# Two small products per step: from one VectorE instruction of two columns to ScalarE copies of one column each

## The chip, the cores and the metric

One NeuronCore of a Trainium2 chip runs the whole program. Its engines are named as in the profile: PE (TensorE matmul), PEld (TensorE weight load), DVE (VectorE), ACT (ScalarE), POOL (GpSimd), SP (SyncE, which here only issues transfers). An engine name with a q is its instruction queue issuing DMAs. The metric is the device time of one execution in microseconds; the median of several executions is compared. For this kernel a change is told from no change when it is over about 0.2%, some 8 us.

## The reference

A transformer block of depth 2 (FFN, mixer, FFN) on 512 tokens of width 1024 is followed by a second block, whose last part is a product-key expert layer ("PEER"). The change touches only that part. Cut to it:

```python
scores = einsum("thpd,hpkd->thpk", query, sub_keys)      # 8 heads, 2 halves, 128 keys
...                                                      # top 16 of each, then top 16 pairs
gate = softmax(best)                                     # 512 tokens x 8 heads x 16 experts
def block_fn(tb, ib, gb):
    act = gelu(einsum("td,thkd->thk", tb, u_tab[ib]))    # u_tab, v_tab: 16384 rows of 1024
    return einsum("thk,thkd->td", gb * act, v_tab[ib])
```

Everything is float32. Each token picks 128 of 16384 experts; an expert is one row of `u_tab` and one of `v_tab`.

## The kernel before

**Two ways through the experts.** For 416 of the 512 tokens (`DENSE`) the kernel computes all experts: PE multiplies the tokens by the whole table `u` ("ahead" tiles), ACT takes the gelu into `stage` and stores it to `s_store` in HBM; later groups of 512 experts read it back (`s_in`) with their gates (`g_in`), DVE multiplies the two (`weighed`), the product is split into a high part (`w_mix_hi`, ACT) and a low part (`w_mix_lo`, DVE), and PE multiplies them by the table `v`. For the other 96 tokens (`FETCHED`) only the chosen rows are fetched, with indirect DMAs from POOL's queue: one fetch brings 128 rows of `u` and `v` (1 MB) into `fetched`, one expert slot per partition. 64 of these tokens have 64 slots per partition, 2 for each of the 32 groups (`PER_GROUP`); the other 32 tokens are the "late" ones with 32 slots, 2 for each of 16 late steps.

**A late step** `s` (`score_late`, `gelu_late`, `add_late`): DVE takes the dot products of two fetched rows with the token (`late_score`, line L3116), ACT takes their gelu (`late_gelu`, L1290), DVE multiplies the two columns by their gates (`late_factor`, L3122) and adds two scaled `v` rows to a total in PSUM (L3126). There are three sets of two `fetched` buffers, so POOL may issue the fetches of step `s + 3` when the two adds of step `s` are done. The late steps run in a window in which PE computes the last 14 ahead tiles, 28 rows of work (a row fills one PSUM bank).

**A group** `g` (`early_step` on ACT, `early_group` on DVE) does the same to two fetched slots with `slot_score` (L3090), `slot_gelu` (L1263), `slot_factor` (L3098) and `fetched_sum` (L3104), between the products `weighed` (L3064) and `w_mix_lo` (L3071). Groups 1 to 30 stand in loops on every engine.

**Weights** come as 331 tiles of 128x2048 in two buffers `raw`. SP loads a tile when POOL is done with the one that was there; ACT copies it rounded into `w_hi` (`split_hi`, L730); POOL subtracts, in four pieces of 512 columns, into `w_lo` (L563); PE waits for the pieces. Each product is then three matmuls (L1362 to L1364).

**What sets the order.** Each engine runs a list written by hand. On ACT, in the window, the gelu of late step `s` is placed after row `ceil(3 + 1.4 s)`:

```python
for row in range(2 * (AHEAD_TILES - WINDOW_AT)):
    n = WINDOW_AT + row // 2
    stage_row(n, row % 2)             # gelu of a PSUM bank, L1168
    if row % 2:
        store_tile(n)                 # DMA s_store, then split_hi of the tile after next
    while s < LATE_STEPS and 3 + 1.4 * s <= row:
        gelu_late(s)
        s += 1
    if row == 2 * (AHEAD_TILES - WINDOW_AT) - 3:
        ...
        load_group(0)                 # DMAs g_in (L1248) and s_in (L1250)
```

On POOL the tile subtractions of the window are placed between the fetches: `fetch_late(s)` first, its two waits included, then `low_tile`. `c.step(ins)` means that the engine waits for its own instruction through a semaphore before it goes on.

Of the kernel before, what the change touches and what calls it, by code (L numbers as in the profile page):

```python
# [23 lines left out]
ALU = mybir.AluOpType  # L24
ACT = mybir.ActivationFunctionType
# [54 lines left out]
PER_GROUP = SLOTS // GROUPS  # L80
# [56 lines left out]
def build(nc, x_in, weights, gains, small, pool_w, consts, rope, second, level_masks,  # L137
# [3 lines left out]
    with stack:  # L141
# [564 lines left out]
        def _(act):  # L706
# [384 lines left out]
            def experts():  # L1091
# [167 lines left out]
                def gelu_fetched(g, i=None):  # L1259

                    at = since("slots_scored") + LATE_SLOTS + PER_GROUP * (g + 1)
                    act.wait_ge(sem("slots_scored"), at if i is None else i * (2 * PER_GROUP) + at)
                    c_sg.up(act.activation(slot_gelu[:, g % 2, :], slot_score[:, g % 2, :], ACT.Gelu))  # L1263
# [12 lines left out]
                def looped(trips, g, body):  # L1276

                    with act.Fori(0, trips) as i:
                        c_wh.loop(i, 2 * EG)
                        c_sg.loop(i, 2)  # L1280
                        body(g, i)
                        body(g + 1, i)
                    for c in (c_wh, c_sg):
                        c.end(trips)

                def gelu_late(s):

                    act.wait_ge(sem("slots_scored"), since("slots_scored") + 2 * (s + 1))
                    c_sg.up(act.activation(late_gelu[:, s % 2, :], late_score[:, s % 2, :], ACT.Gelu))  # L1290

                s = 0
# [978 lines left out]
        def _(dve):  # L2271
# [625 lines left out]
            def experts():  # L2897
# [195 lines left out]
                def factor_fetched(g, i=None):  # L3093

                    done = since("slots_gelu") + LATE_STEPS + g + 1
                    dve.wait_ge(sem("slots_gelu"), done if i is None else i * 2 + done)
                    at = g if i is None else i * 2 + g
                    local.step(dve.tensor_tensor(slot_factor[:, g % 2, :], slot_gelu[:, g % 2, :], slot_gate[:, at, :],  # L3098
                                                 ALU.mult))
# [19 lines left out]
                def add_late(s):  # L3119

                    dve.wait_ge(sem("slots_gelu"), since("slots_gelu") + s + 1)
                    local.step(dve.tensor_tensor(late_factor[:, s % 2, :], late_gelu[:, s % 2, :], late_gate[:, s, :],  # L3122
                                                 ALU.mult))
# [5 lines left out]
                def early_group(g, i=None):  # L3129
# [8 lines left out]
                    factor_fetched(g, i)  # L3138
# [3 lines left out]
                def looped(trips, g, body):  # L3142

                    with dve.Fori(0, trips) as i:
# [4 lines left out]
                        local.loop(i, 2)  # L3149
                        body(g, i)  # L3150
                        body(g + 1, i)
                    for c in (c_wg, c_wl, c_ss, c_fa, local):
                        c.end(trips)
# [175 lines left out]
```

## Time and profile before

| | |
|---|---|
| median of 3 runs | 3894.67 us (3893.44 to 3897.62) |
| the profiled execution | 3893.74 us, span 3891.9 us |
| PE busy | 3771.2 us (97%) |
| DVE busy | 2111.6 us (54%) |
| ACT busy | 1399.0 us (36%) |
| POOL busy | 1978.0 us (51%) |
| granted TensorE clock, mean | 0.985 |
| late window | about 3118 to 3270 us of the span |
| groups | about 3278 to 3874 us |

The span runs from the first to the last instruction of the profiled execution. Busy shares are means over stages with different limits; the change lies in the last fifth of the span, so views of those stretches are read below. In a row of a view, "idle before <- X" is how long the engine had done nothing before the instruction and what ended that.

### The profile page before, as it was taken

The numbers are of one execution on the slowest core, as the hardware profiler recorded it, in microseconds if no ns is written. First come the engines' busy times: TensorE is split into PE (matmuls) and PEld (weight loads), VectorE is DVE, ScalarE is ACT, GpSimd is POOL, SyncE is SP. The second block draws the span as 40 slices with busy tenths as digits, with TensorE's granted clock in tenths as the row PEclk, the third lists the DMA queues.
The fourth block names the chain that finished last, engine by engine and source line by source line (L and its number), as shares of the span: only waits on it lengthen the run. The fifth ranks groups of instructions, "written<-read, shape, count | busy, mean of one in ns | idle before, by whom it ended". The sixth has DMA issues, their size and how long they took to land.

```text
span 3891.9 us, 57381 instructions
## 1 busy us (share of the span) xinstructions
PE 3771.2 (97%) x21920; PEld 3290.5 (85%) x21920; DVE 2111.6 (54%) x3552; ACT 1399.0 (36%) x2131; POOL 1978.0 (51%) x1520
## 2 busy tenths in 40 slices
PE   8999999999999999999999978999999987999998
PEld 7888778888888887788877767889999987999998
DVE  3212555220322056432124855439899968999997
ACT  4222253222322133432232433334477722333332
POOL 4444424444444442444443322546644465888885
PEclk9999999999999999999999988999999998999999
DMA  3222212222222221222223210234456699888885
GB/s 140 97 97 100 77 64 98 97 97 97 95 94 94 104 88 58 92 92 97 98 103 76 44 36 24 99 108 157 154 206 209 226 381 357 326 319 324 323 319 189
DMA packets 160292, 570.02 MB, mean 146 GB/s; under 512 B 19456, under 2 KB 85248, under 8 KB 105344
## 3 DMA queue, kind: packets, MB, share of 16 engines
q1 hardware_dynamic: 49392, 351.29, 25.7%
q10 hardware_dynamic: 96912, 115.76, 8.7%
q0 software_dynamic: 13824, 100.67, 6.3%
q8 instruction: 116, 1.90, 0.2%
q14 instruction: 48, 0.39, 0.0%
HBM read 510.93 MB, written 56.66 MB: 146 GB/s over the span
## 4 chain that ended last, share of the span: by engine, by line
issue 34%; POOL 26%; PE 24%; DVE 13%; ACT 1%; ACTq 1%; DMA 0%; POOLq 0%; DVEq 0%
POOL w_lo L563 25%; PE bank L1362 7%; PE bank L1364 7%; PE bank L1363 7%; DVE g_buf L3043 3%; DVE hot_parts L3025 2%; DVE hot_first L3026 1%; DVE hot_parts L3031 1%; DVE bank L3126 1%; DVE late_factor L3122 1%; DVE fetched L3116 1%; POOL fetched L657 1%; ACT w_hi L730 1%; DVE gk L2601 0%; PE bank L1904 0%
## 5 line engine op out<-in xcount | busy, mean ns | idle before, releaser
L563 POOL TENSOR_TENSOR w_lo<-raw,w_hi 128x512 fp32r<-128x512 f32 x1324 | 1807.6, 1396 | 1722.4 <-ACT w_hi L730 1695.0
L1362 PE MATMUL bank<-h_hi,w_hi 128*128 128x512 f32 (+1 forms) x3232 | 1235.9, 382 | 35.8 <-POOL w_lo L563 22.9
L1363 PE MATMUL bank<-h_lo,w_hi 128*128 128x512 f32 (+1 forms) x3232 | 1222.1, 378 | 0.0
L1364 PE MATMUL bank<-h_hi,w_lo 128*128 128x512 f32 (+1 forms) x3232 | 1222.1, 378 | 0.0
L730 ACT ACTIVATE w_hi<-raw 128x2048 fp32r<-128x2048 f32 x331 | 632.7, 1911 | 832.0 <-PE bank L1364 765.4
L1362 PEld LDWEIGHTS bank<-h_hi,w_hi 128*128 128x128 f32 x3232 | 609.9, 189 | 132.5 <-POOL w_lo L563 34.1
L1363 PEld LDWEIGHTS bank<-h_lo,w_hi 128*128 128x128 f32 x3232 | 610.1, 189 | 89.7 <-issue 3.4
L1364 PEld LDWEIGHTS bank<-h_hi,w_lo 128*128 128x128 f32 x3232 | 609.4, 189 | 88.8
L1362 PE MATMUL bank<-w_mix_hi,w_hi 128*128 128x416 f32 x1024 | 363.3, 355 | 16.0 <-DVE w_mix_lo L3071 15.0
L1364 PE MATMUL bank<-w_mix_hi,w_lo 128*128 128x416 f32 x1024 | 361.8, 353 | 0.0
L1363 PE MATMUL bank<-w_mix_lo,w_hi 128*128 128x416 f32 x1024 | 358.9, 350 | 0.0
L2318 DVE SCALAR_TENSOR_TENSOR x<-bank,x 128x512 f32<-128x512 f32 x56 | 38.1, 680 | 451.1 <-PE bank L1364 451.1
L1364 PE MATMUL bank<-act_hi,w_lo 128*128 (+1 forms) x704 | 274.1, 389 | 0.0
L1362 PE MATMUL bank<-act_hi,w_hi 128*128 (+1 forms) x704 | 274.1, 389 | 0.0
L1363 PE MATMUL bank<-act_lo,w_hi 128*128 (+1 forms) x704 | 274.1, 389 | 0.0
L2354 DVE TENSOR_TENSOR up_s<-bank,rstd 128x512 f32<-128x512 f32 x88 | 60.8, 691 | 381.6 <-PE bank L1364 381.3
L765 ACT ACTIVATE act_hi<-up_s 128x512 f32 (+1 forms) x88 | 55.6, 632 | 458.7 <-DVE up_s L2356 458.7
L1362 PEld LDWEIGHTS bank<-w_mix_hi,w_hi 128*128 128x128 f32 x1024 | 192.9, 188 | 24.0 <-issue 17.6
L3071 DVE TENSOR_TENSOR w_mix_lo<-weighed,w_mix_hi 128x416 fp32r<-128x416 f32 x128 | 199.7, 1560 | 6.9 <-ACT w_mix_hi L1257 3.0
L1363 PEld LDWEIGHTS bank<-w_mix_lo,w_hi 128*128 128x128 f32 x1024 | 193.4, 189 | 2.7
L1364 PEld LDWEIGHTS bank<-w_mix_hi,w_lo 128*128 128x128 f32 x1024 | 193.0, 189 | 1.3
L3064 DVE TENSOR_TENSOR weighed<-s_in,g_in 128x416 f32<-128x416 f32 x128 | 156.6, 1243 | 13.2 <-DMA s_in<-s_store 11.0
(430 smaller groups left out, 4416.4 us busy)
## 6 DMA issues: line engine op xcount, KB each, us to landing
raw<-weights SPq DMA_DIRECT2D x331, 1024.0 KB, 4.8
s_store<-stage ACTq DMA_DIRECT2D x64, 416.0 KB, 4.7
g_store<-g_buf ACTq DMA_DIRECT2D x8, 3328.0 KB, 15.4
g_in<-g_store ACTq DMA_DIRECT2D x32, 832.0 KB, 6.7
s_in<-s_store ACTq DMA_DIRECT2D x32, 832.0 KB, 8.2
x<-x_in SPq DMA_DIRECT2D x4, 512.0 KB, 8.5
out<-x SPq DMA_DIRECT2D x8, 256.0 KB, 2.2
q_mask<-rows ACTq DMA_DIRECT2D x6, 256.0 KB, 4.3
```

The costliest lines, as they stand in the source:

```text
L563: pool.tensor_tensor(w_lo[:, slot, cols], raw[:, slot, cols], w_hi[:, slot, cols].bitcast(F32), ALU.subtract).then_inc(lo_written, 1)
L657: pool.indirect_dma_start(out=fetched[b][:, :, :].rearrange("p a d -> p (a d)"), out_offset=None, in_=expert_rows, in_offset=bass.Indirect ...
L730: act.activation(w_hi[:, slot, :], raw[:, slot, :], ACT.Copy).then_inc(hi_written, 1)
L765: c_act_hi.up(act.activation(act_hi[:, at, :], prod[:, :], ACT.Copy))
L1362: pe.matmul(out_ap, w_hi[:, slot, cols], m_hi, start=start, stop=False)
L1363: pe.matmul(out_ap, w_hi[:, slot, cols], m_lo, start=False, stop=False)
L1364: return pe.matmul(out_ap, w_lo[:, slot, cols], m_hi, start=False, stop=stop)
L2354: c_us.step(dve.tensor_tensor(up_s[:, :], banks[up_bank][:, :], rstd[:, :], ALU.mult))
L3025: local.up(dve.tensor_tensor(parts[:, :, 0:P], every, over_keys(chosen[:, 0]), ALU.is_equal))
L3043: ins = dve.tensor_reduce(g_buf[:, c % 2, :, at:at + 2], both, AX_X, ALU.add)
L3064: c_wg.up(dve.tensor_tensor(chunked(weighed[:, e % 2, :]), chunked(s_in[:, slot, e, :]), g_in[:, slot, :, e, :], ALU.mult))
L3071: c_wl.step(dve.tensor_tensor(w_mix_lo[:, g % 2, e, :], weighed[:, e % 2, :], w_mix_hi[:, g % 2, e, :].bitcast(F32), ALU.subtract))
```

## The change

The gate product leaves DVE. After each gelu of two columns, ACT waits for its own result and then writes the factor as two copies of one column, each scaled by the gate of its slot through a per-partition operand; the semaphore on which DVE waited for the gelu is raised by the second copy. DVE has no product and no wait for its own product any more; `await_factor` is the bare wait.

```diff
                     act.wait_ge(sem("slots_scored"), at if i is None else i * (2 * PER_GROUP) + at)
-                    c_sg.up(act.activation(slot_gelu[:, g % 2, :], slot_score[:, g % 2, :], ACT.Gelu))
+                    act_local.step(act.activation(slot_gelu[:, g % 2, :], slot_score[:, g % 2, :], ACT.Gelu))
+                    at = g if i is None else i * 2 + g
+                    for j in range(PER_GROUP):
+                        ins = act.activation(slot_factor[:, g % 2, j:j + 1], slot_gelu[:, g % 2, j:j + 1], ACT.Copy,
+                                             scale=slot_gate[:, at, j:j + 1])
+                    c_sg.up(ins)
...
                     act.wait_ge(sem("slots_scored"), since("slots_scored") + 2 * (s + 1))
-                    c_sg.up(act.activation(late_gelu[:, s % 2, :], late_score[:, s % 2, :], ACT.Gelu))
+                    act_local.step(act.activation(late_gelu[:, s % 2, :], late_score[:, s % 2, :], ACT.Gelu))
+                    for j in range(2):
+                        ins = act.activation(late_factor[:, s % 2, j:j + 1], late_gelu[:, s % 2, j:j + 1], ACT.Copy,
+                                             scale=late_gate[:, s, j:j + 1])
+                    c_sg.up(ins)
...
-                def factor_fetched(g, i=None):
+                def await_factor(g, i=None):
 
                     done = since("slots_gelu") + LATE_STEPS + g + 1
                     dve.wait_ge(sem("slots_gelu"), done if i is None else i * 2 + done)
-                    at = g if i is None else i * 2 + g
-                    local.step(dve.tensor_tensor(slot_factor[:, g % 2, :], slot_gelu[:, g % 2, :], slot_gate[:, at, :],
-                                                 ALU.mult))
...
                     dve.wait_ge(sem("slots_gelu"), since("slots_gelu") + s + 1)
-                    local.step(dve.tensor_tensor(late_factor[:, s % 2, :], late_gelu[:, s % 2, :], late_gate[:, s, :],
-                                                 ALU.mult))
```

On ACT, at the end of the late window, the list of before reads as follows (`z_read` is the semaphore that counts the scores, and `s_ahead_done` and `tile_used` count PE's rows):

```order
1271 L1290 ACTIVATE late_gelu<-late_score 128x2 [waits z_read]
1272 L1168 ACTIVATE stage<-bank 128x416 [waits s_stored0,s_ahead_done]
1273 L1290 ACTIVATE late_gelu<-late_score 128x2 [waits z_read]
1274 L1168 ACTIVATE stage<-bank 128x416 [waits tile_used]
1275 L1173 DMA s_store<-stage 128x832 [waits s_staged]
1276 L730 ACTIVATE w_hi<-raw 128x2048 [waits tile_used,tile_landed1]
1277 L1248 DMA g_in<-g_store 128x8x208 [waits gates_stored1,gates_stored0]
1278 L1250 DMA s_in<-s_store 128x2x832
```

and that of the change:

```order
1299 L1296 ACTIVATE late_gelu<-late_score 128x2 [waits z_read]
1300 L1298 ACTIVATE late_factor<-late_gelu,late_gate 128x1 [waits act_local]
1301 L1298 ACTIVATE late_factor<-late_gelu,late_gate 128x1
1302 L1168 ACTIVATE stage<-bank 128x416 [waits s_stored0,s_ahead_done]
1303 L1296 ACTIVATE late_gelu<-late_score 128x2 [waits z_read]
1304 L1298 ACTIVATE late_factor<-late_gelu,late_gate 128x1 [waits act_local]
1305 L1298 ACTIVATE late_factor<-late_gelu,late_gate 128x1
1306 L1168 ACTIVATE stage<-bank 128x416 [waits tile_used]
1307 L1173 DMA s_store<-stage 128x832 [waits s_staged]
1308 L730 ACTIVATE w_hi<-raw 128x2048 [waits tile_used,tile_landed1]
1309 L1248 DMA g_in<-g_store 128x8x208 [waits gates_stored1,gates_stored0]
1310 L1250 DMA s_in<-s_store 128x2x832
```

Nothing but the two copies per gelu, the first with a wait on ACT's own semaphore, has come in; the places of the gelus, of `stage`, of `w_hi` and of the first group's two loads are the same, and no load of a function table is added.

On DVE, at the last two late steps (`v_new_written` counts what ACT hands over, `dve_local` is DVE's wait for itself, `x_written2` counts the adds; the number behind `fetched` tells the buffer), before:

```order
1815 L3122 TENSOR_TENSOR late_factor<-late_gelu,late_gate 128x2 [waits v_new_written]
1816 L3126 SCALAR_TENSOR_TENSOR bank<-fetched_193,late_factor,bank 128x1024 [waits x_written2,dve_local]
1817 L3126 SCALAR_TENSOR_TENSOR bank<-fetched_194,late_factor,bank 128x1024 [waits x_written2]
1818 L3116 SCALAR_TENSOR_TENSOR fetched_195,late_score<-fetched_195,bank 128x1024 [waits fetched_landed2]
1819 L3116 SCALAR_TENSOR_TENSOR fetched_196,late_score<-fetched_196,bank 128x1024 [waits fetched_landed3]
1820 L3122 TENSOR_TENSOR late_factor<-late_gelu,late_gate 128x2 [waits v_new_written]
1821 L3126 SCALAR_TENSOR_TENSOR bank<-fetched_195,late_factor,bank 128x1024 [waits x_written2,dve_local]
```

and of the change:

```order
1801 L3131 SCALAR_TENSOR_TENSOR bank<-fetched_193,late_factor,bank 128x1024 [waits x_written2,v_new_written]
1802 L3131 SCALAR_TENSOR_TENSOR bank<-fetched_194,late_factor,bank 128x1024 [waits x_written2]
1803 L3123 SCALAR_TENSOR_TENSOR fetched_195,late_score<-fetched_195,bank 128x1024 [waits fetched_landed2]
1804 L3123 SCALAR_TENSOR_TENSOR fetched_196,late_score<-fetched_196,bank 128x1024 [waits fetched_landed3]
1805 L3131 SCALAR_TENSOR_TENSOR bank<-fetched_195,late_factor,bank 128x1024 [waits x_written2,v_new_written]
```

The product is gone and the wait for ACT has moved to the first add.

## Rows read from the trace of the kernel before

**Rows 1.** Three stretches: length, busy PE, PEld, DVE, ACT, POOL, clock, DMA share, GB/s.

```profile
3150.00:3256.00 106.00, 93.46 (x472) 91.01 (x471) 94.84 (x87) 30.65 (x43) 73.18 (x66) 0.95 1.01 408
3256.00:3264.00 8.00, 8.00 (x44) 7.88 (x43) 7.66 (x11) 0.61 (x2) 6.81 (x6) 1.00 0.53 201
...
3290.00:3860.00 570.00, 569.02 (x2991) 557.57 (x2991) 543.34 (x466) 189.57 (x218) 465.65 (x305) 1.00 0.83 312
```

**Rows 2.** Waits by engine, 3110 to 3300 us: total us, times, longest us.

```profile
ACT late_gelu L1290 <- DVE fetched L3116: 50.8, 14, 5.9
...
PE bank L1362 <- POOL w_lo L563: 20.2, 4, 7.7
...
PE bank L1362 <- DVE w_mix_lo L3071: 15.0, 1, 15.0
```

**Rows 3.** DVE's instruction groups, 3157 to 3257 us: busy us, mean ns, idle before.

```profile
L3122 DVE TENSOR_TENSOR late_factor<-late_gelu,late_gate 128x2 f32<-128x2 f32 x13 | 34.2, 2632 | 10.6 <-ACT late_gelu L1290 10.6
L3126 DVE SCALAR_TENSOR_TENSOR bank<-fetched,late_factor,bank 128x1024 f32<-128x1024 f32 x26 | 33.5, 1290 | 0.9
L3116 DVE SCALAR_TENSOR_TENSOR fetched<-fetched,bank 128x1024 f32<-128x1024 f32 x25 | 29.5, 1215 | 0.0
```

**Rows 4.** Timeline around two late steps: start, us, instruction, idle before.

```profile
3235.53 0.16 DVE L3122 TENSOR_TENSOR late_factor<-late_gelu,late_gate 128x2 f32<-128x2 f32 x1 [0.27 <-ACT late_gelu L1290]
3235.73 2.62 DVE L3126 SCALAR_TENSOR_TENSOR bank<-fetched,late_factor,bank 128x1024 f32<-128x1024 f32 x2
...
3239.57 4.98 POOL L563 TENSOR_TENSOR w_lo<-raw,w_hi 128x512 fp32r<-128x512 f32 x4
...
3240.65 0.20 ACT L1290 ACTIVATE late_gelu<-late_score 128x2 f32<-128x2 f32 x1 [4.74 <-DVE fetched L3116]
...
3240.89 3.69 DVE L3122 TENSOR_TENSOR late_factor<-late_gelu,late_gate 128x2 f32<-128x2 f32 x1 [0.27 <-ACT late_gelu L1290]
```

**Rows 5.** ACT's groups by shape, whole span: with and without a per-partition scale.

```profile
L1193 ACT ACTIVATE hot_parts<-hot_parts,gate_hi 128x128 fp32r<-128x128 f32 x416 | 129.8, 388 | 56.6 <-DVE hot_parts L3031 56.6
...
L1045 ACT ACTIVATE prod_y<-bank 128x128 f32<-128x128 f32 x32 | 8.6, 277 | 48.6 <-PE bank L1944 48.2
...
L1290 ACT ACTIVATE late_gelu<-late_score 128x2 f32<-128x2 f32 x16 | 3.2, 202 | 50.8 <-DVE fetched L3116 50.8
```

**Rows 6.** A stretch of 10 us in the late window, columns as in the first group.

```profile
3160.00:3170.00 10.00, 10.00 (x55) 10.00 (x54) 9.66 (x10) 3.15 (x4) 7.90 (x8) 1.00 1.02 426
```

**Rows 7.** DMA issues, 3190 to 3250 us: median us from issue to landing.

```profile
fetched<-expert_rows,late_at POOLq DMA_INDIRECT x16, 8.5
```

**Rows 8.** Timeline, last late fetch to first group: POOL, DVE, ACT, ACT's queue.

```profile
3247.49 0.94 POOL L657 DMA_INDIRECT fetched<-expert_rows,late_at  x1 [0.37 <-DVE bank L3126]
...
3262.24 1.21 DVE L3116 SCALAR_TENSOR_TENSOR fetched<-fetched,bank 128x1024 f32<-128x1024 f32 x1
...
3264.64 0.20 ACT L1290 ACTIVATE late_gelu<-late_score 128x2 f32<-128x2 f32 x1 [5.55 <-DVE fetched L3116]
...
3266.51 2.96 ACTq L1250 DMA_DIRECT2D s_in<-s_store  x1
...
3278.04 1.94 DVE L3064 TENSOR_TENSOR weighed<-s_in,g_in 128x416 f32<-128x416 f32 x2 [8.09 <-DMA s_in<-s_store]
```

**Rows 9.** Timeline of one group: DVE, then two rows of ACT.

```profile
3615.56 0.82 DVE L3098 TENSOR_TENSOR slot_factor<-slot_gelu,slot_gate 128x2 f32<-128x2 f32 x1 [0.34 <-DVE w_mix_lo L3071]
...
3612.06 0.20 ACT L1263 ACTIVATE slot_gelu<-slot_score 128x2 f32<-128x2 f32 x1 [0.59 <-DVE fetched L3090]
...
3617.61 1.92 ACT L730 ACTIVATE w_hi<-raw 128x2048 fp32r<-128x2048 f32 x1 [5.34 <-PE bank L1364]
```

**Rows 10.** Waits by engine in the groups, 3300 to 3860 us.

```profile
ACT w_hi L730 <- PE bank L1364: 200.3, 41, 6.7
...
PEld bank L1362 <- POOL w_lo L563: 4.5, 11, 0.5
```

**Rows 11.** Timeline, PE, the longest of its waits for `w_lo`.

```profile
3142.25 0.71 PE L1362 MATMUL bank<-h_hi,w_hi 128*128 128x416 f32 x1 [7.71 <-POOL w_lo L563]
```

More of the change, by code:

```diff
@@ L1280, in looped @@
                         c_sg.loop(i, 2)
+                        act_local.loop(i, 2)
                         body(g, i)
                         body(g + 1, i)
-                    for c in (c_wh, c_sg):
+                    for c in (c_wh, c_sg, act_local):
                         c.end(trips)
@@ L3137, in early_group @@
                             score_fetched(g, e, i)
-                    factor_fetched(g, i)
+                    await_factor(g, i)
                     for j in range(PER_GROUP):
@@ L3148, in looped @@
                             c.loop(i, 2 * PER_GROUP)
-                        local.loop(i, 2)
                         body(g, i)
                         body(g + 1, i)
-                    for c in (c_wg, c_wl, c_ss, c_fa, local):
+                    for c in (c_wg, c_wl, c_ss, c_fa):
                         c.end(trips)
```

## Prediction

> **What bounds the kernel now.** I read three views in this order: the stretches, the waits, the timeline.
>
> The stretches [rows 1] cut the last fifth of the span into parts with different limits. In the groups, 3290 to 3860 us, PE is busy 569.02 of 570 us at full clock: PE bounds them, and what DVE or ACT saves there is worth nothing unless PE waited for it. In the late window before them PE is not the bound: it is busy 93.46 of 106 us, DVE 94.84, and the DMA share is 1.01. Two limits lie close together there, DVE's chain and the DMA engines. From 3256 to 3264 us the DMA share falls to 0.53.
>
> The waits [rows 2] say where PE's idle time comes from: 20.2 us for weights that POOL had not split, and 15.0 us in one piece for the first group's `w_mix_lo`, between the last ahead row and the first group. ACT stands 50.8 us before late gelus, waiting for DVE's dot products. So DVE's chain paces ACT, and through the order on ACT and POOL also PE.
>
> DVE's groups in the window [rows 3] show what is odd: 13 factors of two columns take 34.2 us, 2632 ns each, more than the 26 adds of 1024 columns (33.5 us). The timeline [rows 4] shows why. The factor at 3235.53 takes 0.16 us. The one at 3240.89 takes 3.69 us and ends at 3244.58, just when POOL's block of four `w_lo` pieces ends (3239.57 + 4.98 = 3244.55). 
>
> The Trainium skill says this too ("SBUF — State Buffer", "Who interferes with whom"): a DVE instruction with two SBUF inputs contends with a GpSimd instruction that reads SBUF, and the loser waits for the whole instruction. By that rule the wait would be one piece, at most 4.98 / 4 = 1.25 us, and DVE would gain 1.2 us per blocked step; the trace shows 3.5 us more than the free factor, across three pieces. The measurement decides, and the sum goes by it.
>
> **The change, part by part.**
>
> *Removed in the window.* 13 factors go: 34.2 us of DVE, of which 13 x 0.16 = 2.1 us is work and 32.1 us is standing behind POOL [rows 3].
>
> *Added in the window.* Per late step ACT waits for its own gelu and makes two copies of one column with a per-partition scale. No row has such a copy. The small gelu takes 202 ns; a per-partition scale is the difference between 388 and 277 ns at 128 columns, 0.11 us [rows 5]. So one copy is some 0.31 us: two are 0.31 us if they overlap wholly and 0.62 if not at all. I take 0.5, since both are independent, plus a hop that DVE's own step (0.04 us between factor and add [rows 4]) also had. A step that was blocked gets 3.69 + 0.04 - 0.5 = 3.2 us shorter, a free one 0.3 to 0.4 us longer. For the 13 steps: 34.2 + 0.5 - 6.5 = about 28 us less in DVE's chain.
>
> The Trainium skill speaks against the move: "ScalarE: Activation LUTs", "Rules for kernel authors", puts multiplication on VectorE, and its section "What ACT_TABLE_LOAD costs" prices an ACTIVATE at 186 ns plus 0.83 ns a column plus 93 ns per pointer operand, back-to-back ones overlapping by 93 ns. An estimate from that page is 0.47 us for two copies, so by it alone each step would be 0.3 us longer than with a free factor; it leaves out what POOL does to the factor.
>
> *What of the 28 us reaches the end.* Very little, I think, because the DMA engines stand next in line. From 3150 to 3256 us they moved 408 GB/s at a share of 1.01 [rows 1], and the best 10 us of the window 426 at 1.02 [rows 6]. All that moves in it (32 fetches, the weight tiles, the stores) must still move before the first group. 106 us x 408 / 426 = 101.5 us: at most 4.5 us to be had there, nothing at the other end, and I take 0, since the share says that no engine was idle and the difference is in what was being moved.
>
> What is free is the hole after it. Fetches land 8.5 us after issue [rows 7]. The last late one is issued at 3247.49, so its rows are there at about 3256; DVE gets to them only at 3262.24, 6.2 us later [rows 8]. With 28 us out of its chain DVE will have caught up and wait for the landing instead. The last gelu (3264.64) and the load of the first group's `s_in` (3266.51) come earlier by as much as the hole allows. In the 8 us from 3256 the DMA share is 0.53: 8 x 0.47 = 3.8 us of free DMA time [rows 1]. I take 3.8 us of the 6.2: the same bytes then land with 3.8 us less idle time, and `s_in`, on which DVE waited 8.09 us until 3278.04, lands that much earlier. PE's 15.0 us wait keeps its length, because the ahead rows before it move as well: PE's 20.2 us of waits for POOL, which stood behind DVE's adds, give way. If they don't, row 25 (the one ahead of the loads on ACT) holds the load back; that is the lower end, 0.
>
> *The groups.* DVE loses a factor and its wait, 0.82 + 0.34 us in the one shown [rows 9]; ACT gains two copies. DVE then waits for the copies instead: gelu at 3612.06 + 0.20, copies to 3612.8, with 0.3 us more for register work in the loop to 3613.1, while `w_mix_lo` runs to 3615.56 - 0.34 = 3615.22. Hidden by 2 us. Behind the copies on ACT stands `w_hi`, which idles 5.34 us for PE: hidden by 4.8 us. Had those covers gone, 0.8 us for each of 30 groups would be 24 us. What is late in PE's eyes is only POOL's `w_lo`: 4.5 us in 11 waits [rows 10]. I take 0 here.
>
> *Sum.* The profiled execution took 3893.74 us, 0.9 below the median. 3893.74 - 3.8 = 3889.9; against the median 3894.67 - 3.8 = **3890.9 us**, 0.1% faster, which a measurement of this kernel (0.2%, some 8 us) can hardly tell from no change.
>
> **The rivals.**
>
> *Mostly not DMA-bound.* The share of 1.01 may hide slack. Then DVE's chain shortens by its 28 us until PE is the bound: PE's waits for weights are 20.2 us, of which the longest, 7.7 us, ends at 3142 us, ahead of the late steps that this part is about, and stays [rows 11]: 12.5 us. With the hole, 16 us: 3878.5 us. For it: DVE idles 0.0 us before its dot products [rows 3]. Against it: the share, over 106 us.
>
> *Groups with less contention.* One DVE product fewer reads beside POOL, and the 4.5 us in 11 waits for `w_lo` go: 3890.9 - 4.5 = 3886.4 us. For it: `w_lo` and DVE's products slow each other. Against it: only one small product in nine goes.
>
> *Groups with more contention, slower.* DVE now runs some 1 us ahead of POOL in each group, and its long products fall on POOL's pieces where they didn't. PE waits in 11 of about 31 groups, 0.41 us each; if all had such a wait it would be 31 x 0.41 - 4.5 = 8.2 us more. Against the gain of 3.8: 3899.1 us; without that gain 3902.9. It decides from 10 more groups with a wait on. For it: POOL is busy 465.65 of 570 us, and its tile path is what PE waits for. Against it: PE waited at most 0.5 us.
>
> *Nothing.* PE's rows hold the first group's load back, or the longer ACT step does: 3894.7 us.
>
> **How the numbers follow.** The tail gain 0.48, nothing 0.19, less contention in groups 0.12, not DMA-bound 0.11, more contention 0.10. Range: 3883 to 3899. Its upper end takes in nothing and most of more contention; its lower end takes in less contention and the 4.5 us in the window (3890.9 - 4.5 - 4.5 is 3881.9, just under it), and leaves out the case not bound by DMA. Outside it lie 0.11 and half of more contention, with the edges some 0.2. Faster by over 0.2% (below 3886.9) needs the DMA rival or less contention: 0.11 + 0.08, with some of the tail case 0.25. Slower by over 0.2% (over 3902.5): 0.06. The same: 0.69.
>
> **What would show it.** In the profile of the change: no 3.7 us instruction on DVE in the window; DVE's dot products L3123 waiting for DMAs of `fetched`; late steps no closer than 7 us on average; the DMA share 1.0 from 3150 until the first group's loads and no hole near 3256; `weighed` of the first group starting near 3274; PE's waits for `w_lo` in the groups near 4.5 us. It is wrong if late steps come at 6 us or less, if the groups' part (first `weighed` to the end) changes by more than 2 us, or if the copies take over 0.62 us together.

## The result: 0.3% slower

| | before | changed |
|---|---|---|
| median of 7 runs each, us | 3895.78 (3893.44 to 3897.62) | 3908.57 (3906.37 to 3911.01) |
| profiled execution, us | 3893.74 | 3910.09 |
| its span, us | 3891.9 | 3908.3 |
| ratio of the runs | | 1.0032, 95% interval 1.0023 to 1.0042 |

The forecast was 3890.9 us with a range of 3883 to 3899. The time lies 9.6 us above that range, on the side to which I had given 0.06.

Three marks that both traces have cut the 16.4 us between the two spans. The memset ahead of the late steps starts at 3112.14 us before and at 3117.31 after: 5.2 us in code that the change does not touch. From there to the first group's first `weighed` it is 165.90 us before and 161.96 after: 3.9 us less. From there to the end it is 613.9 us before and 629.0 after: **15.2 us more, in the groups and the short tail behind them**.

The changed kernel's stretches, in the columns of [rows 1]:

```profile
3150.00:3256.00 106.00, 98.71 (x494) 96.46 (x493) 68.27 (x84) 36.85 (x70) 77.71 (x69) 0.93 0.99 411
3256.00:3264.00 8.00, 8.00 (x44) 7.86 (x43) 5.36 (x7) 2.12 (x8) 6.96 (x6) 1.00 0.73 278
3290.00:3860.00 570.00, 557.83 (x2908) 542.02 (x2908) 502.33 (x425) 189.92 (x273) 497.15 (x299) 1.00 0.81 310
```

In the late window DVE fell from 94.84 to 68.27 us, and the DMA share hardly moved. In the groups DVE is busy 41 us less than in [rows 1], and POOL, whose work is the same, is busy 31.5 us longer. PE did 2908 matmuls in 570 us where it had done 2991. A group has 8 x 4 x 3 = 96 of them, so a group takes 570 x 96 / 2908 = 18.82 us instead of 18.29; the starts of ACT's `w_hi` give 18.83 and 18.31, the means of 30 groups.

The waits of the changed kernel in the groups, 3290 to 3860 us (total us, times, longest), which answer to [rows 10]:

```profile
ACT w_hi L730 <- PE bank L1374: 294.3, 60, 6.0
...
DVE w_mix_lo L3081 <- ACT w_mix_hi L1257: 56.2, 60, 2.4
PEld bank L1372 <- POOL w_lo L563: 22.7, 30, 0.8
...
PE bank L1372 <- POOL w_lo L563: 12.2, 30, 0.4
```

PE now waits for `w_lo` in every group, 0.4 us each, and its weight loads do so 30 times, 22.7 us in all, where [rows 10] had 11 such waits, 4.5 us. ACT waited for PE ahead of every `w_hi`, 60 of 60. DVE waits for ACT's `w_mix_hi` twice a group (2 times in all before): with the product gone it runs ahead as far as ACT lets it.

The instruction groups of that stretch (busy us, mean ns, idle before) show who got slower. First the kernel before:

```profile
L563 POOL TENSOR_TENSOR w_lo<-raw,w_hi 128x512 fp32r<-128x512 f32 x246 | 382.9, 1586 | 91.2 <-ACT w_hi L730 90.7
...
L3104 DVE SCALAR_TENSOR_TENSOR fetched_sum<-fetched,slot_factor,fetched_sum 128x1024 f32<-128x1024 f32 x62 | 99.4, 1603 | 5.3
```

and the changed one:

```profile
L563 POOL TENSOR_TENSOR w_lo<-raw,w_hi 128x512 fp32r<-128x512 f32 x240 | 423.1, 1795 | 59.5 <-ACT w_hi L730 59.1
...
L3111 DVE SCALAR_TENSOR_TENSOR fetched_sum<-fetched,slot_factor,fetched_sum 128x1024 f32<-128x1024 f32 x60 | 126.1, 2102 | 8.0 <-DVE w_mix_lo L3081 6.9
```

Both sides of one meeting: a `w_lo` piece went from 1586 to 1795 ns, a fetched add, the same instruction on the same shape, from 1603 to 2102 ns.

The timeline of one group of the changed kernel (start, us, instruction, idle before) shows where they meet:

```profile
3598.80 1.92 ACT L730 ACTIVATE w_hi<-raw 128x2048 fp32r<-128x2048 f32 x1 [3.83 <-PE bank L1374]
3600.63 0.53 ACT L1257 ACTIVATE w_mix_hi<-weighed 128x416 fp32r<-128x416 f32 x1
3601.06 0.19 ACT L1263 ACTIVATE slot_gelu<-slot_score 128x2 f32<-128x2 f32 x1
3601.39 0.48 ACT L1266 ACTIVATE slot_factor<-slot_gelu,slot_gate 128x1 f32<-128x1 f32 x2
...
3600.81 7.37 POOL L563 TENSOR_TENSOR w_lo<-raw,w_hi 128x512 fp32r<-128x512 f32 x4
3609.86 6.73 POOL L563 TENSOR_TENSOR w_lo<-raw,w_hi 128x512 fp32r<-128x512 f32 x4 [1.68 <-ACT w_hi L730]
...
3601.19 1.38 DVE L3081 TENSOR_TENSOR w_mix_lo<-weighed,w_mix_hi 128x416 fp32r<-128x416 f32 x1 [0.70 <-ACT w_mix_hi L1257]
3602.81 4.23 DVE L3111 SCALAR_TENSOR_TENSOR fetched_sum<-fetched,slot_factor,fetched_sum 128x1024 f32<-128x1024 f32 x2 [0.24 <-DVE w_mix_lo L3081]
3606.96 2.17 DVE L3074 TENSOR_TENSOR weighed<-s_in,g_in 128x416 f32<-128x416 f32 x2
```

ACT and POOL come to a new tile when PE has left its buffer: `w_hi` at 3598.80, POOL's block of four pieces at 3600.81. The last `w_mix_lo`, both adds and the start of the next `weighed` all lie inside that block, and it takes 7.37 us; a block with nothing of DVE that contends takes 5.0 (4.98 in [rows 4]). PE starts on the tile at its end and hands the buffer back at 3617.62, where ACT's next `w_hi` starts. So a group is the block plus 11.46 us: 18.83. Each group is the same: all 30 intervals between every second `w_hi` are 18.8 or 18.9 us. Before, they ran 18.1, 18.3, 18.5 in turn.

The kernel before in the same stretch, rows of ACT, POOL, DVE and PEld:

```profile
3608.64 0.55 ACT L1257 ACTIVATE w_mix_hi<-weighed 128x416 fp32r<-128x416 f32 x1 [2.65 <-DVE weighed L3064]
3609.10 1.91 ACT L730 ACTIVATE w_hi<-raw 128x2048 fp32r<-128x2048 f32 x1
...
3611.09 6.53 POOL L563 TENSOR_TENSOR w_lo<-raw,w_hi 128x512 fp32r<-128x512 f32 x4
...
3593.37 5.67 DVE L3071 TENSOR_TENSOR w_mix_lo<-weighed,w_mix_hi 128x416 fp32r<-128x416 f32 x1
...
3616.51 3.50 DVE L3104 SCALAR_TENSOR_TENSOR fetched_sum<-fetched,slot_factor,fetched_sum 128x1024 f32<-128x1024 f32 x2
...
3617.67 0.19 PEld L1362 LDWEIGHTS bank<-w_mix_hi,w_hi 128*128 128x128 f32 x1 [0.45 <-POOL w_lo L563]
```

Two things differ. In a group like this one, two of three, the adds begin at 3616.51, 5.4 us into the block of 3611.09, where in the changed kernel they begin 2.0 us into it. And in the third a `w_mix_lo` stands still for a whole block (5.67 us at 3593.37; 11 times over the groups, never in the changed kernel, where the longest takes 1.7); that block takes 5.03 us, and the adds behind it take 2.60 us, as little as anywhere. PE's 11 waits for `w_lo` have another cause than now: for ten of them the tile's `w_hi` had not waited for PE. It had begun late, behind a `w_mix_hi` on ACT, as at 3609.10, and a block of 6.53 us then ended 0.45 us too late. That is one such wait in three groups, and three groups take 0.5 us more than three times the 18.15 us of PE alone (experiment 6).

### The profile page after: what moved, and what is told of

Read it like the earlier page. It is cut to its first block, busy times and chain, and to the rows that moved or that the text cites. A ratio compares the mean times of both kernels' runs of the same rounds, so it can differ in the third digit from the quotient of the medians.

```text
span 3908.3 us, 57457 instructions
## 1 busy us (share of the span) xinstructions
PE 3780.5 (97%) x21920; PEld 3294.4 (84%) x21920; DVE 2044.9 (52%) x3504; ACT 1412.5 (36%) x2227; POOL 2020.6 (52%) x1520
## 4 chain that ended last, share of the span: by engine, by line
issue 35%; POOL 29%; PE 22%; DVE 11%; DMA 1%; ACT 1%; ACTq 1%; POOLq 0%; DVEq 0%; SPq 0%
POOL w_lo L563 28%; PE bank L1372 6%; PE bank L1374 6%; PE bank L1373 6%; DVE g_buf L3053 3%; DVE hot_parts L3035 1%; DVE hot_first L3036 1%; DVE hot_parts L3041 1%; POOL fetched L657 1%; ACT w_hi L730 1%; DMA fetched<-expert_rows,late_at 1%; PE bank L1914 1%; DVE gk L2611 0%; DVE gq L2611 0%; PE bank L2155 0%
## 5 line engine op out<-in xcount | busy, mean ns | idle before, releaser
L563 POOL TENSOR_TENSOR w_lo<-raw,w_hi 128x512 fp32r<-128x512 f32 x1324 | 1858.3, 1436 | 1698.8 <-ACT w_hi L730 1671.4
L1372 PE MATMUL bank<-w_mix_hi,w_hi 128*128 128x416 f32 x1024 | 363.8, 355 | 28.5 <-DVE w_mix_lo L3081 15.7
L1372 PEld LDWEIGHTS bank<-w_mix_hi,w_hi 128*128 128x128 f32 x1024 | 192.7, 188 | 40.9 <-POOL w_lo L563 22.7
L3081 DVE TENSOR_TENSOR w_mix_lo<-weighed,w_mix_hi 128x416 fp32r<-128x416 f32 x128 | 155.1, 1212 | 57.3 <-ACT w_mix_hi L1257 57.1
L2362 DVE TENSOR_TENSOR gate_s<-bank,rstd 128x512 f32<-128x512 f32 x88 | 60.9, 692 | 184.9 <-PE bank L1374 184.6
```

What stands on the lines that cost most here:

```text
L563: pool.tensor_tensor(w_lo[:, slot, cols], raw[:, slot, cols], w_hi[:, slot, cols].bitcast(F32), ALU.subtract).then_inc(lo_written, 1)
L1372: pe.matmul(out_ap, w_hi[:, slot, cols], m_hi, start=start, stop=False)
L2362: c_gs.step(dve.tensor_tensor(gate_s[:, :], banks[gate_bank][:, :], rstd[:, :], ALU.mult))
L3081: c_wl.step(dve.tensor_tensor(w_mix_lo[:, g % 2, e, :], weighed[:, e % 2, :], w_mix_hi[:, g % 2, e, :].bitcast(F32), ALU.subtract))
```

## Experiments

Theory A: the product kept DVE behind POOL in the groups. Without it DVE's long products with both inputs in SBUF, the fetched adds above all, lie deeper inside POOL's block of a tile and stretch it past what PE leaves time for. Its rivals: ACT's copies lengthen ACT's own queue (C) or ACT's order of `w_hi` and `w_mix_hi` makes the 18.83 us (D); the loss is spread over both halves of the change, or comes with the length of the code (B).

All of them use the two marks above: the late window is memset to first `weighed` (165.9 us before, 162.0 changed), a group is every second `w_hi`.

**1. The late steps alone.** The groups' edit is left out.

Against the kernel before:

```diff
-                    c_sg.up(act.activation(late_gelu[:, s % 2, :], late_score[:, s % 2, :], ACT.Gelu))
+                    act_local.step(act.activation(late_gelu[:, s % 2, :], late_score[:, s % 2, :], ACT.Gelu))
+                    for j in range(2):
+                        ins = act.activation(late_factor[:, s % 2, j:j + 1], late_gelu[:, s % 2, j:j + 1], ACT.Copy,
+                                             scale=late_gate[:, s, j:j + 1])
+                    c_sg.up(ins)
...
-                    local.step(dve.tensor_tensor(late_factor[:, s % 2, :], late_gelu[:, s % 2, :], late_gate[:, s, :],
-                                                 ALU.mult))
```

> ScalarE makes the factors of the 13 late steps only; in the groups VectorE multiplies them as before. Theory A (the loss is made in the groups: with the product gone from VectorE, its fetched adds run while GpSimd subtracts a w_lo block, and make GpSimd's tile path longer than TensorE's): the late window keeps its gain of some 4 us, the groups run at their old 18.33 us each, and the time is some 4 us under before, about 3891.5. Rival B (ScalarE's copies and the extra hand-over cost wherever they stand, the late window included): 3895 to 3900. The stage between 2123 and 2401 us of the profile, which no edit touches, was 5 us longer in the profile of the changed kernel: if that is where the code stands in memory, it shows here in part; if it is a matter of the single execution, it comes and goes with no relation to the edits.

Measured: 3891.99 us (11 runs), ratio 0.9989, interval 0.9980 to 0.9998. Late window 164.2 us; groups in the old pattern 18.1, 18.3, 18.5. Theory A's sign and place hold; the time is 3.6 us under before, less than the 0.2% named at the start, though the interval leaves out no change. (The edit takes in all 16 late steps; 13 is the number that [rows 3] shows.)

**2. The groups alone.** The other half.

Against the kernel before:

```diff
-                    c_sg.up(act.activation(slot_gelu[:, g % 2, :], slot_score[:, g % 2, :], ACT.Gelu))
+                    act_local.step(act.activation(slot_gelu[:, g % 2, :], slot_score[:, g % 2, :], ACT.Gelu))
+                    at = g if i is None else i * 2 + g
+                    for j in range(PER_GROUP):
+                        ins = act.activation(slot_factor[:, g % 2, j:j + 1], slot_gelu[:, g % 2, j:j + 1], ACT.Copy,
+                                             scale=slot_gate[:, at, j:j + 1])
+                    c_sg.up(ins)
...
-                    local.step(dve.tensor_tensor(slot_factor[:, g % 2, :], slot_gelu[:, g % 2, :], slot_gate[:, at, :],
-                                                 ALU.mult))
```

> ScalarE makes the factors of the 32 groups only; in the late steps VectorE multiplies them as before. Theory A: the whole loss and none of the gain: groups of 18.83 us instead of 18.33, 15 us more than before, 3909 to 3912, slower than the full change by some 4 us. Rival B (the loss is spread over both parts, or comes from the code's length): nearer to before than the full change is, 3897 to 3905.

Measured: 3906.06 us (6 runs), ratio 1.0029 (1.0016 to 1.0041). The loss is here, and the figures were a miss all the same, for both theories: not 18.83 us a group but a pattern of four, 18.6, 18.1, 18.5, 19.2 (mean 18.6), reached after some seven groups, from the first `weighed` to the end 622.0 us. The blocks for which PE waits in it take 7.1 and 7.5 us. So the same code in the groups can settle in different rhythms; what picks one is not shown. The two halves do not add up either: 10.4 us more and 3.6 less make 6.8, and the whole change cost 12.8.

**3. The change, with an idle product on DVE.**

```diff
     dve.wait_ge(sem("slots_gelu"), ...)
+    local.step(dve.tensor_tensor(idle_out[:, :], slot_gate[:, at, :], slot_gate[:, at, :], ALU.mult))
     add_fetched(g, 0); add_fetched(g, 1)
```

> The full change, and in each group VectorE also makes a product of 128x2 out of SBUF at the place of the old one, whose result nobody reads. Theory A: what cost the time is that VectorE no longer stands still until GpSimd's block is over; the idle product restores that, the groups go back to about 18.33 us each and the time to 3890 to 3893, though this kernel has more instructions than either. Rival C (ScalarE's copies, which stand ahead of w_hi on its queue, lengthen the groups): the idle product changes nothing or adds 0.3 us a group, 3908 to 3918.

Measured: 3890.77 us, ratio 0.9988 (0.9979 to 0.9997). One useless instruction of two columns takes 17 us off the changed kernel. Groups 18.1, 18.3, 18.5 again; ACT makes the factors all the same, so the ACT side is not what cost. The idle product's own times are 0.16 us at least and 0.91 in the median, which is a wait for POOL. Its groups' rows in the stretch 3290 to 3860 us:

```profile
L564 POOL TENSOR_TENSOR w_lo<-raw,w_hi 128x512 fp32r<-128x512 f32 x248 | 385.1, 1583 | 91.3 <-ACT w_hi L731 90.7
...
L3114 DVE SCALAR_TENSOR_TENSOR fetched_sum<-fetched,slot_factor,fetched_sum 128x1024 f32<-128x1024 f32 x62 | 99.4, 1603 | 5.3
```

They are those of the kernel before to within 3 ns. In its timeline a pair of adds takes 2.60 us in one group of three, clear of POOL, and 3.5 us in the others; in the change it is 4.23 us in the group shown above, and nearly the same in all. So the product does not keep the adds clear, only less deep in the block.

**4. The kernel before, with idle copies on ACT.**

```diff
-                    c_sg.up(act.activation(slot_gelu[:, g % 2, :], slot_score[:, g % 2, :], ACT.Gelu))
+                    act_local.step(act.activation(slot_gelu[:, g % 2, :], slot_score[:, g % 2, :], ACT.Gelu))
+                    at = g if i is None else i * 2 + g
+                    for j in range(PER_GROUP):
+                        ins = act.activation(idle_out[:, j:j + 1], slot_gelu[:, g % 2, j:j + 1], ACT.Copy,
+                                             scale=slot_gate[:, at, j:j + 1])
+                    c_sg.up(ins)
```

> The kernel before, with ScalarE's two copies added in each group behind the gelu, with a result that nobody reads; VectorE still makes the product. Rival C: the copies alone lengthen a group by up to their 0.5 us, 3905 to 3911. Theory A: they fall into ScalarE's wait for TensorE and the groups keep 18.33 us, 3894 to 3897.

Measured: 3893.52 us, ratio 0.9993 (0.9984 to 1.0002). This is 0.5 us under the expected band. Rival C falls: the copies are covered.

**5. The changed kernel again.**

> The changed kernel once more, nothing edited. In its first profile the memset ahead of the late steps began at 3117.3 us, in the kernel before at 3112.1, in the four kernels so far between 3111.6 and 3117.6. If that is the scatter of single executions, this profile has another figure in that band and the median stays at 3906 to 3909; if it belongs to this code, the figure is 3117 again. The groups should take 18.83 us each again (theory A gives a fixed pattern, since every group meets the same block).

Measured: 3907.11 us (6 runs), ratio 1.0029 (1.0017 to 1.0042), groups of 18.8 us, late window 163.7 us. The memset started at 3113.1 us, so the 5.2 us ahead of the late steps were that one execution's. Over all 13 profiles of this study it lies between 3111.6 and 3117.6 us, in no order that follows the edits.

**6. The change without its fetched adds.** The fetched slots of the groups are missing from the sum.

```diff
-    scalar_tensor_tensor(fetched_sum, fetched[...][:, 1, :], slot_factor[..., j], fetched_sum, mult, add)
+    tensor_copy(fetched_sum[:, j:j + 1], slot_factor[:, g % 2, j:j + 1])
```

> The full change, with the two fetched adds of each group left out of the computation (a copy of one column gives their signal instead, so the fetched slots of the groups are missing from the sum). Theory A: GpSimd's second w_lo block has no adds beside it, falls from 7.37 us to under 6.5, and each group takes TensorE's own 18.1 us in place of 18.83: 22 us less than the full change, 3884 to 3889. Rival D (the group of 18.83 us is made by ScalarE's order: w_hi of one tile stands ahead of the last w_mix_hi, which stands ahead of w_hi of the next): the order is unchanged, so 3905 to 3909 stays.

**7. The kernel before without its fetched adds**, in the same way.

> The kernel before, with the two fetched adds of each group left out in the same way; VectorE still makes the product. Theory A: the groups go from 18.33 to 18.1 us or so, 3887 to 3890: without the adds the two forms stand within 5 us of each other, so that nearly the whole 13 us between them is the adds' meeting with GpSimd. Rival D: both kernels keep their distance of 13 us.

Measured: 3888.00 us, ratio 0.9980 (0.9971 to 0.9989), for experiment 6, and 3892.03 us, ratio 0.9988 (0.9979 to 0.9997), for 7. Groups of 18.1 to 18.2 us in both, so the distance of 13 us is turned into 4 the other way. Rival D falls as the cause of the 18.83 us: ACT's order is unchanged. The second time is 2 us above what was expected. The groups stretch of experiment 6:

```profile
3290.00:3860.00 570.00, 570.00 (x3025) 562.33 (x3023) 488.74 (x435) 195.70 (x280) 438.73 (x306) 1.00 0.83 310
```

3025 matmuls, 18.09 us a group by this count and 18.15 by the starts of `w_hi`, in both experiments: this is PE with nothing in its way. POOL is busy 438.7 us in place of 497.2. But more has changed than that the adds are gone. A `w_mix_lo` now stands still for a whole block in every group, and the mean of a `w_mix_lo` is 2252 ns in experiment 6 and 2239 in 7, against 1233 in the change; the blocks take 5.04 and 6.73 us in turn. So these two experiments show that the loss needs the adds, and not what a block would take if nothing met it. Experiment 8, which leaves nothing out, is the cleaner test.

**8. The change, with the adds held back.**

```diff
     await_factor(g, i)
+    if i is not None or g > 0:
+        at = PIECES * (v_tile(g - 1) + 3)
+        dve.wait_ge(lo_written, at if i is None else i * (PIECES * 4) + at)
     for j in range(PER_GROUP): add_fetched(g, j)
```

> The full change, and in each group VectorE waits, ahead of its fetched adds, for the end of GpSimd's block of the tile that is under way there (a wait, no instruction). It does what the product did by its blocking. Theory A: the adds no longer lie beside that block, the block falls from 7.37 to some 5.5 us, and the groups go back to 18.1 to 18.4 us: 3884 to 3893. Against it: the held adds and the two weighed behind them then lie beside the other block, now 6.73 us; if that one grows past 7.4 us in turn, the time stays at 3905 or above.

Measured: 3890.00 us (3885.43 to 3893.31, 11 runs), ratio 0.9985 (0.9976 to 0.9994): 5.5 us under before and some 18 under the change. Its timeline of one group:

```profile
3607.45 6.53 POOL L563 TENSOR_TENSOR w_lo<-raw,w_hi 128x512 fp32r<-128x512 f32 x4
3616.30 6.38 POOL L563 TENSOR_TENSOR w_lo<-raw,w_hi 128x512 fp32r<-128x512 f32 x4 [2.32 <-ACT w_hi L730]
...
3614.11 2.61 DVE L3111 SCALAR_TENSOR_TENSOR fetched_sum<-fetched,slot_factor,fetched_sum 128x1024 f32<-128x1024 f32 x2 [2.53 <-POOL w_lo L563]
3616.64 3.28 DVE L3074 TENSOR_TENSOR weighed<-s_in,g_in 128x416 f32<-128x416 f32 x2
```

The block ends at 3613.98, the adds run in the 2.3 us in which POOL waits for ACT, and take 1.3 us each instead of 2.1. The blocks settle at 6.36 and 6.53 us (one of the first took 6.91), and after the first few groups each takes 18.1 to 18.2 us, PE's own time. The time and the groups came out as expected, the block did not: 5.5 us had been expected. It only had to stay under the 6.69 us that PE leaves it (18.15 less 11.46). DVE stands 74.9 us in that wait over the groups, and it costs nothing that the time shows.

**9. The kernel before, with the same hold** ahead of its product.

> The kernel before (VectorE makes all factors), with the same wait ahead of the product and the adds of each group as in hold_adds. It asks what the wait alone is worth. Theory A: the groups are settled by when the adds run, so here too they come to 18.15 us each instead of 18.33 (5 to 6 us less) and the late window stays as before: 3888.5 to 3892, some 2 us above hold_adds, which is what ScalarE's factors bring in the late window. Rival E (the good groups of hold_adds need ScalarE's factors as well): 3894 to 3897.

Measured: 3903.37 us, ratio 1.0018 (1.0008 to 1.0027). Both expectations fall: the hold alone makes the kernel 7 us slower. Its timeline, from the slowest of the 11 executions (3908.26 us):

```profile
3601.46 6.53 POOL L563 TENSOR_TENSOR w_lo<-raw,w_hi 128x512 fp32r<-128x512 f32 x4 [0.52 <-ACT w_hi L730]
3609.80 6.73 POOL L563 TENSOR_TENSOR w_lo<-raw,w_hi 128x512 fp32r<-128x512 f32 x4 [1.80 <-ACT w_hi L730]
...
3608.25 0.16 DVE L3098 TENSOR_TENSOR slot_factor<-slot_gelu,slot_gate 128x2 f32<-128x2 f32 x1 [2.64 <-POOL w_lo L563]
3608.55 3.62 DVE L3104 SCALAR_TENSOR_TENSOR fetched_sum<-fetched,slot_factor,fetched_sum 128x1024 f32<-128x1024 f32 x2
3612.10 3.28 DVE L3064 TENSOR_TENSOR weighed<-s_in,g_in 128x416 f32<-128x416 f32 x2
...
3617.64 0.55 ACT L1257 ACTIVATE w_mix_hi<-weighed 128x416 fp32r<-128x416 f32 x1 [1.68 <-DVE weighed L3064]
3618.10 1.90 ACT L730 ACTIVATE w_hi<-raw 128x2048 fp32r<-128x2048 f32 x1
```

The product and its step take 0.30 us of the gap (3608.25 to 3608.55). The second add is then still running when POOL's next block starts at 3609.80, and the pair takes 3.62 us instead of 2.61. Everything on DVE is later by that, the third `w_mix_hi` too, and the next `w_hi` (3618.10) stands behind it on ACT without waiting for PE. Groups: 18.6 us against the 18.15 of experiment 8. So ScalarE's factors are worth something in the groups once the adds are held. That it is the 0.3 us of the product that decides is read from these timelines; no run changed it alone.

**10. The change with one add of two.** The first fetched slot of each group is missing from the sum.

```diff
     c_fa.held()
+    if j == 0:
+        c_fa.up(dve.tensor_copy(fetched_sum[:, j:j + 1], slot_factor[:, g % 2, j:j + 1]))
+        return
```

> The full change with the first of the two adds of each group left out of the computation (a copy of one column gives its signal). In the profiles a group lasts 11.46 us plus GpSimd's longer block (18.83 with 7.37), and never under the 18.15 us of TensorE. One add alone should lengthen the block by half as much as two: 6.2 to 6.7 us, at or under the 6.69 us at which TensorE takes over, so groups of 18.15 to 18.3 us and a time of 3886 to 3893. If each add costs its share of the time in a straight line instead (no floor), the groups take some 18.5 us and the time is 3897 to 3900.

Measured: 3887.72 us, ratio 0.9979 (0.9970 to 0.9989), groups of 18.1 to 18.2 us. The straight line falls, the floor holds, but the block did not shrink by half as expected. The instruction groups of its groups stretch:

```profile
L563 POOL TENSOR_TENSOR w_lo<-raw,w_hi 128x512 fp32r<-128x512 f32 x248 | 366.1, 1509 | 114.9 <-ACT w_hi L730 114.4
...
L3081 DVE TENSOR_TENSOR w_mix_lo<-weighed,w_mix_hi 128x416 fp32r<-128x416 f32 x124 | 277.6, 2239 | 25.4 <-ACT w_mix_hi L1257 21.5
L3114 DVE SCALAR_TENSOR_TENSOR fetched_sum<-fetched,slot_factor,fetched_sum 128x1024 f32<-128x1024 f32 x31 | 41.1, 1325 | 1.1
```

`w_lo` is as fast as with no add at all (1509 against 1501 ns), the add that is left takes 1325 ns, clear of POOL, and `w_mix_lo` has gone from 1233 ns in the change to 2239. The meeting has moved, as in experiments 6 and 7: one `w_mix_lo` a group now stands still behind a whole block, which leaves the block short, and holds DVE off until it is over. How the block grows with the adds is therefore not shown by it.

**11. The change, with an idle product in the late steps.**

```diff
     dve.wait_ge(sem("slots_gelu"), since("slots_gelu") + s + 1)
+    local.step(dve.tensor_tensor(idle_out[:, :], late_gate[:, s, :], late_gate[:, s, :], ALU.mult))
```

> The full change, and in each of the 16 late steps VectorE also makes a product of 128x2 out of SBUF at the old one's place, with a result that nobody reads. In the groups nothing is added, so they keep 18.83 us. Theory F (what the late window gained is the blocking of the product, some 2 us from the memset to the first weighed, the rest of its 34 us being covered by the transfers): that stretch goes back from 161.6 to 164.2 to the 164.7 to 165.9 us of the kernels with the product, and the time to 3908 to 3912. Rival G (the gain of 2 us is from something else in the change): the stretch stays at 162 to 164 us.

Measured: 3915.99 us (5 runs, 3912.49 to 3916.42), ratio 1.0051 (1.0036 to 1.0065). The late window is back at 166.2 us, as theory F had it and above its bound by 0.3. DVE's group, 3160 to 3260 us:

```profile
L3130 DVE TENSOR_TENSOR idle_out<-late_gate 128x2 f32<-128x2 f32 x12 | 29.4, 2449 | 9.4 <-ACT late_factor L1299 9.4
```

Twelve idle products take 29.4 us, as the thirteen real ones of [rows 3] took 34.2. The time is 4 us above the expected band. The groups keep 18.8 us, the profiled execution was the fastest of the five, and no view shows where the other runs spend 3.5 us more: that stays open.

The late window in all 13 profiles: with a product on DVE 165.9, 164.7, 165.9, 164.2, 165.8 and 166.2 us, mean 165.5; without it 162.0, 164.2, 163.5, 163.7, 164.0, 162.6 and 162.2, mean 163.2. The gain is 2.3 us; the two sets touch at 164.2.

## Why the prediction was wrong

**The late window: the size came near, the place of the gain was half missed.** The late steps' rows of the changed kernel, DVE's groups from 3157 to 3257 us, against [rows 3]:

```profile
L3131 DVE SCALAR_TENSOR_TENSOR bank<-fetched,late_factor,bank 128x1024 f32<-128x1024 f32 x27 | 34.8, 1289 | 30.2 <-ACT late_factor L1298 29.8
L3123 DVE SCALAR_TENSOR_TENSOR fetched<-fetched,bank 128x1024 f32<-128x1024 f32 x26 | 31.3, 1217 | 8.0 <-DMA fetched<-expert_rows,late_at 7.9
```

and three rows of its timeline, against [rows 8]:

```profile
3263.06 0.48 ACT L1298 ACTIVATE late_factor<-late_gelu,late_gate 128x1 f32<-128x1 f32 x2
...
3264.92 4.61 ACTq L1250 DMA_DIRECT2D s_in<-s_store  x1
...
3263.58 2.61 DVE L3131 SCALAR_TENSOR_TENSOR bank<-fetched,late_factor,bank 128x1024 f32<-128x1024 f32 x2 [0.79 <-ACT late_factor L1298]
```

The 34.2 us of factors are gone, and DVE idles 30.2 us for ACT and 8.0 for the fetches instead. Two copies take 0.48 us; I had taken 0.5. The Trainium skill ("ScalarE: Activation LUTs", "What ACT_TABLE_LOAD costs") gives 0.47 by my estimate, and the trace agrees.

Of 28 us removed from DVE's chain 2.3 reach the end; I had said 3.8, and the one pair of profiles shows 3.9. I had put all of it into the hole from 3256 to 3264 us and nothing into the transfers ahead of it. Counted from the memset, these two stretches lie 5.17 us later in the changed kernel:

```profile
3155.17:3261.17 106.00, 98.71 (x494) 96.40 (x493) 67.46 (x82) 37.37 (x72) 78.05 (x69) 0.94 1.00 417
3261.17:3269.17 8.00, 8.00 (x44) 7.86 (x43) 5.80 (x6) 3.00 (x5) 4.66 (x5) 1.00 0.85 314
```

At a share of 1.0 as before the DMA engines moved 417 GB/s instead of the 408 of [rows 1]. That brings the same bytes 106 x (1 - 408 / 417) = 2.3 us earlier. In the same stretch all six kernels with a product on DVE moved 403 to 411 GB/s, all seven profiles without one 416 to 418: about the 2.3 us of the mean. The hole did not close: over the 16 us that begin 140 us after the memset, in slices of 1 us, the missing share adds up to 3.9 us before and 2.4 changed, and to 3.4 and 2.9 in the means of the two sets. In the one pair, more than half of the gain thus came from the term for which I had written "I take 0", and that the sum came near 3.8 was in part luck. Why the same share carries 2% more bytes is not shown.

PE's waits for `w_lo` between 3110 and 3300 us went from 20.2 to 14.7 us, and the 15.0 us one kept its length (15.7), as I had said. That the transfers cover the rest of the 28 us fits the share; no run here took bytes away to test it. The rival "mostly not DMA-bound" gave 16 us and is out.

**The step that failed is "I take 0 here", for the groups.** It held three errors.

First, its cover was right and it was the wrong question. I showed that the copies hide behind `w_mix_lo` and behind ACT's wait for PE, and they do (experiment 4). What I took to be free was the other side: DVE's lost 0.82 + 0.34 us. With them, in two groups of three, the adds began 5.4 us into POOL's block and not 2.0, and in the third behind it. A product that nobody reads brings the old groups back (experiment 3), and a hold in its place works better still (experiment 8).

Second, I named the mechanism as the rival "more contention, slower" and mis-sized it. I priced it by the old waits, 31 x 0.41 - 4.5 = 8.2 us. But the old waits were of another kind: a block of 6.53 us that began late, behind a `w_mix_hi` on ACT. They say nothing of a block that itself grows past what PE leaves it. It became 7.37 us, and with the 11.46 us around it the price is (18.83 - 18.31) x 30 = 15.6 us, near the 15.2 between the two profiles. An upper estimate of the block could have been had from rows of before: 4.98 us [rows 4] with two adds of 1.3 us wholly inside it [rows 3] is 7.6 us if they shut each other out. A chance of 0.10 was too low for that.

Third, "PE bounds them" was read from 569.02 of 570 us busy. Ends of matmuls are modelled, so that sum cannot tell 18.15 us a group from 18.31. The count can: 2991 matmuls in [rows 1] against the 3025 of experiment 6. The groups ran 1% above PE's time already, one in three waiting for a block that ACT and DVE had made late, so anything that moved DVE against POOL could move the time either way. The rival "less contention" (3886.4) was the other face of this; it is what experiment 8 reached, at 3890.0.

**What I said would show it** did: first `weighed` to the end changed by more than 2 us, which I had named as what makes the forecast wrong, and the waits for `w_lo` in the groups went from 4.5 to 22.7 us for the weight loads and from none that the view shows to 12.2 us for the matmuls.

**What is still open.** Which rhythm the groups settle into is not explained by the code of the groups alone: the changed kernel keeps to 18.83 us in three profiles (its two and experiment 11), and with the late steps as before it falls into the pattern of four. Why a DVE product sometimes stands still for a whole block and sometimes shares with it (below) is open too.

## What to carry to other kernels

An instruction that does nothing but wait may be holding two engines apart. Before you take it away from an engine that is not the bound, ask what then starts earlier, and whether it lands on something on the path: here 1.2 us of DVE time saved in a group (0.82 + 0.34) made it 0.5 us longer, and a bare wait in its place brought more than that back.

Judge whether an engine is the bound by instructions done per microsecond against its best stretch, not by its busy share alone. The same goes for the DMA engines: at a share of 1.0 throughout, 2% more bytes went through once DVE's chain was shorter.

Halve a change that touches two places before you judge it: its late half was worth 0.1%, its other half cost 0.3%.

## What the runs showed of the hardware

A DVE instruction with both inputs in SBUF and GpSimd's `w_lo` meet in two ways. In one, DVE stands still until the whole block of four pieces is over and the block keeps 5.0 us (a `w_mix_lo` of 5.67 us beside a block of 5.03 in the kernel before); in the other both go on, slower (adds of 2.10 us instead of 1.29 and a block of 7.37 in the changed one). The Trainium skill ("SBUF — State Buffer", "Who interferes with whom") calls the port pair that DVE and GpSimd share an exclusive lock, for which a DVE instruction with two SBUF inputs contends with a GpSimd instruction that reads SBUF. The trace agrees that they hold each other up, but the wait isn't bounded by one instruction: the same `w_mix_lo` of 416 columns takes 0.58, 1.68 or 5.69 us in one kernel (hold_adds: least 0.578, most 5.685), and 5.69 less the 0.58 of its own work is 5.1 us, about the length of a whole block of four pieces. In both ways the shapes are the same; the runs do not show what chooses.

A tiny product is not spared: those of 128x2 took 2.4 to 2.6 us on average in the late window (3.69 us in [rows 4]), for 0.16 us of work.
